# Seven half products in place of eight for three quarters of an MLP's first matrix

## The chip, the cores and the metric

The kernel runs on one core of one Trainium2 chip. A core has TensorE (matrix products, from SBUF into PSUM), VectorE and ScalarE (elementwise work on SBUF and PSUM), GpSimd (elementwise work on SBUF) and SyncE, which issues most of the transfers from HBM. The metric is device time in microseconds (us), from start to end of one execution; here the median of three runs.

## The reference

Two layers of a decoder trunk over 512 tokens of width 1024, in float32. Each layer has a mixer with four branches, a cross attention into 256 memory tokens, and a squared-ReLU MLP with 4096 hidden channels. The change is in the MLP:

```python
h = rmsnorm(x, norm_mlp[l])
x = x + sq_relu_mlp(h, mlp_w1[l], mlp_w2[l])

def sq_relu_mlp(h, w1, w2):
    return jnp.square(jax.nn.relu(h @ w1)) @ w2      # w1: 1024 x 4096, w2: 4096 x 1024
```

## The kernel before

Activations lie transposed: channels in 8 tiles of 128 partitions (index k), the 512 tokens along the free axis. Each matrix product in float32 is made of three in a reduced format (fp32r). Every operand is split into a high half and the low rest, and a product is high by high, high by low and low by high. A product is one weight load of 128x128 and one matmul that streams 512 columns.

**Blocks and units.** All large matrices go through one ring of 9 weight units (`RING`, L151). A unit holds 256 rows by 256 columns, as four squares of 128x128, and comes with one transfer of 256 KB, issued by SyncE when the unit nine earlier has been used (`wait_for_place`, L470). ScalarE writes the unit's high half (`feed`, L1322), GpSimd subtracts it from the raw unit in place, in two instructions (L637, L638), and TensorE uses both (`parts`, L647). A block is four units: it makes two output tiles of 128 channels by 512 tokens in the two banks of a PSUM set, G[0] or G[1], which the blocks take in turn. A unit of a block is 12 products, a block 48. Before the first product of a block TensorE waits until both banks of its set were released (`gemm_free`).

**The MLP** is cut into four quarters of 1024 hidden channels. Block `up{q}_{c}` makes two hidden tiles of quarter q, block `down{q}_{c}` adds quarter q's share to two tiles of x. The order is up0, up1, down0, up2, down1, up3, down2, down3, of four blocks each (L131). The norm's factor per token is not applied to the operands `h_hi` and `h_lo`, but to the hidden tiles: VectorE takes max(product, 0) times the factor into `UPX[0]` (L2533), ScalarE squares it into `UPX[1]` and copies it to the high half (L1798, L1799), VectorE makes the low half (L2537). The factor itself is there only after the first block: TensorE sums the squares behind up0_0 (L1268), ScalarE makes the factor of it (`factors(2)`, L1784). The results of `down` blocks are added to x by VectorE (`residual`, L2419).

**What sets the order.** Each engine has its own queue, written out by hand, and works it off in order. ScalarE feeds weight units in the gaps of its other work: ahead of the two outputs of block b it feeds up to five units (`LEAD`, L153) past that block's last (`feed_past`, L1330). Each instruction of VectorE and ScalarE waits for the one before it on its own engine.

Of the kernel before, what the change touches and what calls it, by code (L numbers as in the profile page):

```python
# [115 lines left out]
def block_order():  # L116
# [14 lines left out]
    order += ups[0] + ups[1] + downs[0] + ups[2] + downs[1] + ups[3] + downs[2] + downs[3]  # L131
# [32 lines left out]

def is_last(u):
    name, part = UNITS[u]
    return part == units_of(name) - 1
# [16 lines left out]
    s5_y_done=2, s5_glu_done=2, s5_ge_value=2, s5_ge_high=2, attn_sc_done=4, attn_pt_done=8, attn_o_done=8, rstd_ready=8, hi_ready=24,  # L184
# [3 lines left out]
    mlstm_mex_ready=1, mlstm_within=4, s5_xp_zero=2, s5_ct_ready=2, s5_bt_ready=4, s5_sq=2, s5_tanh=2,  # L188
    s5_val_ready=2, mghi_ready=8, attn_mm_hi=8, sq_ready=24, attn_kqv_hi=20, attn_kt_ready=8, attn_q_ready=8, attn_vm_ready=4,
    attn_p_exp=16, attn_pt_hi=8, attn_pt_ready=8, attn_ohi_ready=8, up_relu=32, up_hi=32, hx_ready=8, h_ready=24, hg_decay_ready=5,  # L190
# [3 lines left out]
    s5_cp_ready=2, s5_xp_ready=2, s5_kk_ready=6, s5_cl_ready=1, s5_x_ready=1, s5_ys_ready=2, s5_poly=2, s5_ge_ready=2,  # L194
# [5 lines left out]
def build(nc, ins, out):  # L200
# [7 lines left out]
    with ctx:  # L208
# [5 lines left out]
        Hhi = sb("h_hi", [P, KC, SEQ], F32R)  # L214
        Hlo = sb("h_lo", [P, KC, SEQ], F32R)
        merged_at = nc.sbuf_base
# [85 lines left out]
        gemm_free = [sem(f"gemm_free{i}") for i in range(2)]  # L302
# [67 lines left out]
        def ones_and_values(rows, t, h):  # L370
# [43 lines left out]
                   "cl_ready", "u_ready", "w_done", "u4_in", "x_ready", "y_done", "ge_value", "ge_high", "ys_ready", "sq", "poly", "tanh",  # L414
# [35 lines left out]
        MHID = [[YS_R[:, 16 * b + 8 * p:16 * b + 8 * p + 8, :] for p in range(2)] for b in range(2)]  # L450
# [19 lines left out]
        def wait_for_place(eng, u):  # L470

            layer, unit = divmod(u - RING, NUNIT)
            if is_last(unit):
                n = layer * NBLOCK + BLOCK["g_v" if UNITS[unit][0] == "r_i" else UNITS[unit][0]]
                eng.wait_ge(gemm_done[n % 2], 2 * (n // 2) + 2)
            else:
                eng.wait_ge(unit_used, INNER[u - RING])
# [164 lines left out]
        def _(pe):  # L642
# [4 lines left out]
            def parts(name, hi, lo, kind="fm", n=SEQ, ready=None, ready_at=0):  # L647
# [5 lines left out]
                if used:  # L653
                    pe.wait_ge(gemm_free[s], 2 * used)
                u0, units, kcs = first_unit(name), units_of(name), 1 if kind == "wide" else 2
                for un in range(units):
# [4 lines left out]
                    for reg in range(nt):  # L661
                        for k in range(kcs):
# [37 lines left out]
            def token_values():  # L700
# [18 lines left out]
                if used0:  # L719
                    pe.wait_ge(gemm_free[s0], 2 * used0)  # L720
# [3 lines left out]
                if used1:  # L724
                    pe.wait_ge(gemm_free[s1], 2 * used1)
# [189 lines left out]
            for L in range(DEPTH):  # L915
# [254 lines left out]
                pe.wait_ge(gemm_free[s], 2 * used)  # L1170
# [93 lines left out]
                for q in (0, 1):  # L1264
                    for c in range(4):
                        gemm(f"up{q}_{c}", *H, ready=h_ready if (q, c) == (0, 0) else None, ready_at=16)
                        if (q, c) == (0, 0):
                            norm(2)  # L1268

                def down(q):  # L1270
                    hb = MHID[q % 2]
                    for c in range(4):
                        gemm(f"down{q}_{c}", lambda k: hb[0][:, k, :], lambda k: hb[1][:, k, :],
                             ready=uplo if c == 0 else None, ready_at=8 * q)

                down(0)
                for c in range(4):
                    gemm(f"up2_{c}", *H)
                down(1)
                for c in range(4):  # L1280
                    gemm(f"up3_{c}", *H)
                down(2)
                down(3)

# [10 lines left out]
            for t in (0, 1):  # L1295
                n = DEPTH * NBLOCK - 2 + t
                pe.wait_ge(gemm_free[n % 2], 2 * (n // 2) + 2)
# [17 lines left out]
        def _(act):  # L1315
# [6 lines left out]
            def feed(upto):  # L1322

                for u in range(fed[0], min(upto, ALL_UNITS)):
                    act.wait_ge(raw_in[u % RING], COME[u])
# [57 lines left out]
            def values_out(name):  # L1383
                s, used = psum_set(name)
                for b in range(2):
# [5 lines left out]
                    act.nop().then_inc(gemm_free[s], 1)  # L1391

            def banks(name):
# [3 lines left out]
                for b in range(2):  # L1397
                    act.wait_ge(gemm_done[s], 2 * used + b + 1)
                    yield b, G[s][b], gemm_free[s]
# [14 lines left out]
            def gate(n, c):  # L1414
# [3 lines left out]
                for b in range(2):  # L1418
# [4 lines left out]
                    act.nop().then_inc(gemm_free[s], 1)  # L1423
# [1163 lines left out]
```

## Time and profile before

| | us |
|---|---|
| median of three runs (1978.82 to 1979.11) | 1979.01 |
| the profiled execution's own time | 1979.01 |
| its span, first to last instruction | 1977.2 |
| TensorE busy | 1954.3 (99%) |
| GpSimd busy | 1086.8 (55%) |
| VectorE busy | 959.0 (49%) |
| ScalarE busy | 913.8 (46%) |

Busy time is the union of the instructions' spans. A matmul's span includes its fill and drain and overlaps the next one's, so that the distance of two starts, not the span of one, is what a matmul costs. "Idle before, releaser" names what ended an engine's idle time. The MLP of layer 0 runs from about 643 to 991 us, that of layer 1 from about 1615 to 1963 us.

### The profile page before, as it was taken

How to read it: one execution, taken by the hardware profiler on the slowest of the kernel's cores; microseconds unless marked ns; L12 is line 12 of the kernel's file. 1: busy time of each engine (PE TensorE's matmuls, PEld its weight loads, DVE VectorE, ACT ScalarE, POOL GpSimd, SP SyncE). 2: the span in 40 equal slices, each digit the busy share in tenths (PEclk: the TensorE clock that was granted, in tenths of full speed). 3: DMA queues.
4: the chain of work that ended last, by engine and by line, in shares of the span. 5: the costliest groups of instructions: out<-in, count | busy, mean ns of one | idle time of the engine just before them, and what ended most of it. 6: DMA issues, size and time to landing. Idle time of an engine off the chain costs nothing.

```text
span 1977.2 us, 30720 instructions
## 1 busy us (share of the span) xinstructions
PE 1954.3 (99%) x11859; PEld 1619.5 (82%) x11859; DVE 959.0 (49%) x1430; ACT 913.8 (46%) x1560; POOL 1086.8 (55%) x1356
## 2 busy tenths in 40 slices
PE   7999999999999999999999999999999999999998
PEld 6778788888888888888887877888798888888887
DVE  5887778856153321211258787786631532211212
ACT  6754645345454542333355546353554544333323
POOL 5565564946835454546464555368585445545451
PEclk9999999999999999999999999999999999999999
DMA  6323333333422333333333233233343233333331
GB/s 188 110 74 86 81 81 87 91 104 112 142 86 81 97 97 96 96 96 98 99 97 81 70 86 81 75 91 86 118 136 110 75 95 97 96 96 97 98 99 70
DMA packets 197262, 190.72 MB, mean 96 GB/s; under 512 B 23738, under 2 KB 190204, under 8 KB 196732
## 3 DMA queue, kind: packets, MB, share of 16 engines
q1 hardware_dynamic: 196252, 186.66, 32.5%
q8 instruction: 94, 1.54, 0.3%
q10 hardware_dynamic: 864, 2.10, 0.3%
q14 instruction: 52, 0.43, 0.1%
HBM read 184.51 MB, written 3.15 MB: 95 GB/s over the span
## 4 chain that ended last, share of the span: by engine, by line
PE 95%; ACT 2%; DVE 2%; issue 0%; DMA 0%; POOL 0%; SPq 0%; DVEq 0%; ACTq 0%
PE gemm L644 87%; PE mix L644 7%; DVE work L1826 1%; ACT w_hi L1327 1%; PE mix L1223 0%; DVE h_lo L1835 0%; DVE work L1835 0%; DMA work<-in_norm_mix_dram 0%; DVE gate_t L1835 0%; PE mix L885 0%; ACT work L1492 0%; PE mix L1119 0%; ACT work_split L1485 0%; DVE work L2217 0%; ACT work L1447 0%
## 5 line engine op out<-in xcount | busy, mean ns | idle before, releaser
L637 POOL TENSOR_TENSOR w_lo<-w_raw,w_hi 128x256 fp32r<-128x256 f32 x676 | 567.2, 839 | 862.3 <-ACT w_hi L1327 861.9
L644 PE MATMUL gemm<-work_split,w_hi 128*128 128x512 f32 (+1 forms) x2064 | 604.2, 377 | 2.8 <-ACTq L1423 2.8
L638 POOL TENSOR_TENSOR w_lo<-w_raw,w_hi 128x256 fp32r<-128x256 f32 x676 | 571.3, 845 | 0.0
L644 PE MATMUL gemm<-h_hi,w_hi 128*128 128x512 f32 x1440 | 568.6, 395 | 1.1 <-DVE h_lo L1835 1.1
L644 PE MATMUL gemm<-h_lo,w_hi 128*128 128x512 f32 x1440 | 560.9, 389 | 0.0
L644 PE MATMUL gemm<-h_hi,w_lo 128*128 128x512 f32 x1440 | 560.8, 389 | 0.0
L1327 ACT ACTIVATE w_hi<-w_raw 128x512 fp32r<-128x512 f32 x676 | 384.7, 623 | 232.2 <-DMA w_raw<-in_mlp_w_dram 186.2
L644 PEld LDWEIGHTS gemm<-work_split,w_hi 128*128 128x128 f32 x2064 | 378.6, 188 | 74.2 <-ACTq L1423 3.7
L644 PE MATMUL gemm<-work_split,w_lo 128*128 128x512 f32 (+1 forms) x1032 | 388.0, 376 | 0.0
L644 PEld LDWEIGHTS gemm<-h_hi,w_hi 128*128 128x128 f32 x1440 | 270.3, 188 | 65.7 <-issue 6.6
L644 PEld LDWEIGHTS gemm<-h_hi,w_lo 128*128 128x128 f32 x1440 | 270.3, 188 | 57.1
L644 PEld LDWEIGHTS gemm<-h_lo,w_hi 128*128 128x128 f32 x1440 | 270.5, 188 | 55.0 <-issue 1.0
L1826 DVE TENSOR_TENSOR x_t<-x_t,gemm 128x512 f32<-128x512 f32 x96 | 66.0, 687 | 356.6 <-PE gemm L644 355.6
L644 PEld LDWEIGHTS gemm<-work_split,w_lo 128*128 128x128 f32 x1032 | 194.3, 188 | 35.4
L1835 DVE SCALAR_TENSOR_TENSOR gate_t<-gemm,work 128x512 f32<-128x512 f32 x64 | 44.3, 692 | 183.7 <-PE gemm L644 166.8
L1798 ACT ACTIVATE gate_t<-gate_t 128x512 f32<-128x512 f32 x64 | 40.5, 632 | 190.9 <-DVE gate_t L1835 190.9
L1826 DVE TENSOR_TENSOR work<-work 128x512 f32<-128x512 f32 (+5 forms) x134 | 120.4, 899 | 14.1 <-ACT work L1528 6.5
L1422 ACT ACTIVATE gate_t<-gemm 128x512 f32<-128x512 f32 x52 | 31.1, 599 | 141.1 <-PE gemm L644 140.7
L644 PEld LDWEIGHTS mix<-work 64*64 64x64 f32 (+4 forms) x3136 | 76.9, 129 | 17.7 <-issue 14.4
L1835 DVE SCALAR_TENSOR_TENSOR work_split<-gate_t,work_split 128x512 fp32r<-128x512 f32 x64 | 45.4, 710 | 88.9 <-ACT work_split L1799 88.9
L644 PE MATMUL mix<-work 64*64 64x64 f32 (+8 forms) x3136 | 84.2, 231 | 0.9 <-DVE work L1835 0.6
L644 PE MATMUL gemm<-w_hi,work_split 128*128 128x512 f32 x192 | 66.1, 398 | 1.5 <-POOL w_lo L638 1.5
(318 smaller groups left out, 1643.6 us busy)
## 6 DMA issues: line engine op xcount, KB each, us to landing
w_raw<-in_mlp_w_dram SPq DMA_DIRECT2D x256, 256.0 KB, 2.7
w_raw<-in_w_in_dram SPq DMA_DIRECT2D x208, 256.0 KB, 2.7
w_raw<-in_xattn_w_kv_dram SPq DMA_DIRECT2D x64, 256.0 KB, 3.0
w_raw<-in_w_branch_dram SPq DMA_DIRECT2D x32, 256.0 KB, 2.6
w_raw<-in_w_out_dram SPq DMA_DIRECT2D x32, 256.0 KB, 2.6
w_raw<-in_xattn_w_q_dram SPq DMA_DIRECT2D x32, 256.0 KB, 2.8
w_raw<-in_xattn_w_o_dram SPq DMA_DIRECT2D x32, 256.0 KB, 2.7
w_raw<-in_w_in_dram SPq DMA_DIRECT2D x32, 128.0 KB, 4.1
```

The costliest lines, as they stand in the source:

```text
L637: pool.tensor_tensor(lo[:, 0:half], raw[:, 0:half], hi[:, 0:half].bitcast(F32), ALU.subtract)
L638: pool.tensor_tensor(lo[:, half:], raw[:, half:], hi[:, half:].bitcast(F32), ALU.subtract).then_inc(split_ready, 1)
L644: return pe.matmul(o, w, a, start=start, stop=stop, skip_group_check=True)
L1327: act.activation(hi, raw, ACT.Copy).then_inc(split_hi, 1)
L1422: do(act.activation(t[:, b, :], G[s][b][:, :], ACT.Tanh, scale=0.5), th_ready)
L1798: do(act.activation(UPX[1], UPX[0], ACT.Square), up_a)
L1826: do(dve.tensor_tensor(o, a, b, op), s)
L1835: do(dve.scalar_tensor_tensor(out=o, in0=a, scalar=sc, in1=b, op0=op0, op1=op1), s)
```

## The change

For quarters one to three of the first matrix, a unit's 256x256 square of weights and the matching 256 channels by 512 tokens of the operand are each taken as 2x2 blocks, and their product is made by Winograd's form of Strassen's algorithm: seven products of half the columns (256 tokens each) in place of eight. Each is still three matmuls in fp32r. Sums over the four units of a block are kept in the four banks of the PSUM tensor `mix` (M[0] to M[3]), the results are put together once a block. Quarter zero is made as before.

- **Token operands** (once a layer, TMhi/TMlo and TXhi/TXlo): for each pair j of channel tiles VectorE multiplies x by the gain and the norm factor (two instructions of 512) and makes four sums of 256 (`turned_sums`); ScalarE copies 1024 and 768 elements into the high half (`turned_hi`); VectorE makes the low half, 1024 and 768 elements (`turned_low`). The four pairs are worked in with the hidden tiles 0 to 4 of quarter zero (`TURNS`).
- **Weight operands** (each unit of the 12 blocks): four sums of 128 elements on VectorE (`weight_sums`), one of them in place; a ScalarE copy of 384 elements ahead of the unit's own copy; a VectorE split of 384 (`sums_low`).
- **Outputs** (each of the 12 blocks): a ScalarE copy of 256 from M[0], six VectorE additions (`products_out`), then ReLU, square and high half on ScalarE for each of two tiles, low halves on VectorE.
- **Order**: after quarter zero the blocks alternate, up1_0, down0_0, up1_1, down0_1 and so on, and four `down3` blocks end the layer.
- **Release** of PSUM banks has one semaphore for each bank. TensorE waits for the second bank only ahead of the first product that goes into it. Four semaphores of a part of the mixer (`s5`) are merged into two, with the same waits.

```diff
-    order += ups[0] + ups[1] + downs[0] + ups[2] + downs[1] + ups[3] + downs[2] + downs[3]
+    order += ups[0]
+    for q in range(1, 4):
+        for c in range(4):
+            order += [ups[q][c], downs[q - 1][c]]
+    order += downs[3]
...
+        TURNS = [1, 2, 3, 4]
+        SUM_STEPS = [(q, c) for q in range(1, 4) for c in range(4)]
...
# TensorE, parts(): one wait for each bank
-                if used:
-                    pe.wait_ge(gemm_free[s], 2 * used)
+                        if used and un == 0 and reg * 2 % nt == 0:
+                            pe.wait_ge(gemm_free[s][reg * 2 // nt], used)
...
# TensorE, a block of quarters one to three
+                def up_sums(q, c):
+                    s, used = psum_set(f"up{q}_{c}")
+                    for b in range(2):
+                        pe.wait_ge(gemm_free[s][b], used)
+                    u0 = first_unit(f"up{q}_{c}")
+                    for j in range(4):
+                        u = u0 + j
+                        pe.wait_ge(split_ready, u + 1)
+                        pe.wait_ge(*of_layer(ws_split, sum_unit(u % NUNIT) + 1))
+                        if (q, c) == (1, 0):
+                            pe.wait_ge(*of_layer(h_ready, 24 + j + 1))
...
+                        for n, (o, (w_hi, w_lo), (t_hi, t_lo), opens) in enumerate((
+                                (M[0][:, FIRST], w(0), t(0, FIRST), True), (M[0][:, SECOND], ws(1), tx(1), False),
...
+                            mm(o, w_hi, t_hi, start=opens and j == 0, stop=False)
+                            mm(o, w_hi, t_lo, start=False, stop=False)
+                            i = mm(o, w_lo, t_hi, start=False, stop=j == 3)
...
# ScalarE, feed(): a unit of the twelve blocks waits for its sums
+                    d = sum_unit(u % NUNIT)
+                    if d is None:
+                        act.wait_ge(raw_in[u % RING], COME[u])
+                    else:
+                        act.wait_ge(*of_layer(ws_ready, d + 1))
+                        act.activation(SWhi[d % 4], SWraw[d % 4], ACT.Copy)
                     raw, hi, _ = unit_at(u)
                     act.activation(hi, raw, ACT.Copy).then_inc(split_hi, 1)
...
# ScalarE, the MLP
+                def turned_hi(j):
+                    act.wait_ge(*of_layer(hx_ready, 8 + j + 1))
+                    do(act.activation(TMhi[:, 2 * j:2 * j + 2, :], TMraw[:, 2 * j:2 * j + 2, :], ACT.Copy))
+                    do(act.activation(TXhi[j], TXraw[j], ACT.Copy), hi_ready)
...
+                for c in range(4):
+                    feed(min(first_unit(f"up0_{c}") + 4 + LEAD, first_unit("up1_0")))
+                    if c == 3:
+                        feed(first_unit("up1_0") + 4)
+                    for b in range(2):
+                        act.wait_ge(*of_layer(up_v, n + 1))
+                        if n:
+                            act.wait_ge(*of_layer(uplo, n))
+                        do(act.activation(UPX[1], UPX[0], ACT.Square), up_a)
+                        do(act.activation(MHID[0][0][:, 2 * c + b, :], UPX[1], ACT.Copy), uphi)
+                        n += 1
+                        if n in TURNS:
+                            turned_hi(TURNS.index(n))
+                feed_past("up1_0")
+                feed(first_unit("down0_0") + 4)
+                for t, (q, c) in enumerate(SUM_STEPS):
+                    ahead = first_unit("up{}_{}".format(*SUM_STEPS[t + 1])) if t < 11 else first_unit("down3_0")
+                    if t < 11:
+                        feed(ahead + 3)
+                    s, used = psum_set(f"up{q}_{c}")
+                    act.wait_ge(gemm_done[s], 2 * used + 2)
+                    do(act.activation(UPX[0][:, FIRST], M[0][:, FIRST], ACT.Copy), up_a)
+                    feed(ahead + 4)
...
+                    if t < 11:
+                        feed(ahead + 8)
...
# VectorE, the MLP
+                def weight_sums(u):
+                    dve.wait_ge(raw_in[u % RING], COME[u])
+                    d = sum_unit(u % NUNIT)
+                    if d >= 4:
+                        wait_used(dve, u - 8)
...
+                ahead = first_unit("up1_0")
+                for c in range(4):
+                    s, used = psum_set(f"up0_{c}")
+                    if c == 3:
+                        for j in range(4):
+                            weight_sums(ahead + j)
+                            if j:
+                                sums_low(ahead + j - 1)
+                        sums_low(ahead + 3)
+                    for b in range(2):
+                        dve.wait_ge(gemm_done[s], 2 * used + b + 1)
+                        if n:
+                            dve.wait_ge(*of_layer(up_a, n))
+                        stt(UPX[0], G[s][b][:, :], 0.0, R(32)[:, 0, :], ALU.max, ALU.mult, up_v)
+                        dve.nop().then_inc(gemm_free[s][b], 1)
+                        if n in TURNS:
+                            turned_low(TURNS.index(n))
+                        n += 1
+                        if n in TURNS:
+                            turned_sums(TURNS.index(n))
+                        hidden_low(0, c, b, UPX[1])
+                for t, (q, c) in enumerate(SUM_STEPS):
+                    if t:
+                        residual("down{}_{}".format(SUM_STEPS[t - 1][0] - 1, SUM_STEPS[t - 1][1]))
+                    ahead = first_unit("up{}_{}".format(*SUM_STEPS[t + 1])) if t < 11 else None
+                    if ahead:
+                        weight_sums(ahead)
+                        weight_sums(ahead + 1)
+                        sums_low(ahead)
+                        weight_sums(ahead + 2)
+                        sums_low(ahead + 1)
+                    products_out(q, c, n)
+                    if ahead:
+                        weight_sums(ahead + 3)
+                        sums_low(ahead + 2)
+                    hidden_low(q, c, 0, MHRAW[q % 2][:, 2 * c, :])
+                    if ahead:
+                        sums_low(ahead + 3)
+                    hidden_low(q, c, 1, MHRAW[q % 2][:, 2 * c + 1, :])
```

## Rows read from the trace of the kernel before

**Rows 1.** The page, part 1 (busy us, share, instructions) and part 4 (last chain).

```profile
PE 1954.3 (99%) x11859; PEld 1619.5 (82%) x11859; DVE 959.0 (49%) x1430; ACT 913.8 (46%) x1560; POOL 1086.8 (55%) x1356
...
PE 95%; ACT 2%; DVE 2%; issue 0%; DMA 0%; POOL 0%; SPq 0%; DVEq 0%; ACTq 0%
```

**Rows 2.** The waits of TensorE: total us, times, longest us.

```profile
PE gemm L905 <- DMA work<-in_norm_mix_dram: 7.0, 1, 7.0
PE gemm L644 <- ACTq L1423: 2.8, 2, 1.4
```

**Rows 3.** The timeline of TensorE, 533 to 536: start, us, instruction, count.

```profile
533.03 0.39 PE L644 MATMUL gemm<-h_hi,w_hi 128*128 128x512 f32 x1
...
535.75 0.39 PE L644 MATMUL gemm<-h_hi,w_hi 128*128 128x512 f32 x1
```

**Rows 4.** The timeline of VectorE, the MLP's first blocks of layer 0.

```profile
656.08 0.69 DVE L1835 SCALAR_TENSOR_TENSOR gate_t<-gemm,work 128x512 f32<-128x512 f32 x1 [7.89 <-ACT work L1359]
...
664.25 0.69 DVE L1835 SCALAR_TENSOR_TENSOR gate_t<-gemm,work 128x512 f32<-128x512 f32 x1 [2.54 <-PE gemm L644]
666.31 1.60 DVE L1835 SCALAR_TENSOR_TENSOR work_split<-gate_t,work_split 128x512 fp32r<-128x512 f32 x1 [1.36 <-ACT work_split L1799]
```

**Rows 5.** The timeline of ScalarE, the same blocks.

```profile
656.87 0.63 ACT L1798 ACTIVATE gate_t<-gate_t 128x512 f32<-128x512 f32 x1 [0.88 <-DVE gate_t L1835]
...
661.02 2.20 ACT L1327 ACTIVATE w_hi<-w_raw 128x512 fp32r<-128x512 f32 x4
```

**Rows 6.** The timeline of GpSimd, the same blocks.

```profile
661.73 0.75 POOL L637 TENSOR_TENSOR w_lo<-w_raw,w_hi 128x256 fp32r<-128x256 f32 x1 [8.78 <-ACT w_hi L1327]
662.43 0.75 POOL L638 TENSOR_TENSOR w_lo<-w_raw,w_hi 128x256 fp32r<-128x256 f32 x1
```

**Rows 7.** Busy us in one stretch of the MLP: PE, PEld, DVE, ACT, POOL; clock, DMA.

```profile
700.00:800.00 100.00, 100.00 (x443) 82.80 (x442) 19.99 (x30) 35.18 (x59) 50.88 (x72) 1.00 0.32 96
```

**Rows 8.** The timeline of TensorE, attention of layer 0.

```profile
551.39 0.28 PE L644 MATMUL mix<-work_split,merged_split 128*128 128x256 f32 x1
...
553.42 0.28 PE L644 MATMUL mix<-work_split 128*128 128x256 f32 x1
```

**Rows 9.** The timeline of VectorE and GpSimd, 190 to 206, in the mixer.

```profile
190.92 3.39 DVE L1835 SCALAR_TENSOR_TENSOR work<-work,params_all 128x512 f32<-128x512 f32 x3
191.44 1.18 POOL L638 TENSOR_TENSOR w_lo<-w_raw,w_hi 128x256 fp32r<-128x256 f32 x1
...
193.73 1.19 POOL L638 TENSOR_TENSOR w_lo<-w_raw,w_hi 128x256 fp32r<-128x256 f32 x1
...
197.34 0.43 DVE L1826 TENSOR_TENSOR work<-work 128x256 f32<-128x256 f32 x1
...
198.84 0.69 DVE L1826 TENSOR_TENSOR work<-work 128x512 f32<-128x512 f32 x1
...
200.15 2.33 DVE L1835 SCALAR_TENSOR_TENSOR work<-work,params_all 128x512 f32<-128x512 f32 x3
```

**Rows 10.** Groups of ScalarE by form: busy us, mean ns, idle before.

```profile
L1428 ACT ACTIVATE work<-work 128x1024 f32<-128x1024 f32 x12 | 12.7, 1062 | 27.0 <-DVE work L1826 26.9
```

**Rows 11.** TensorE at both ends (timeline), then the granted clock (windows; column PEclk).

```profile
11.77 1.09 PE L885 MATMUL mix<-consts_sb,work 128*128 128x128 f32 x4 [0.86 <-ACT work_split L1485]
...
14.84 0.62 PE L644 MATMUL gemm<-w_lo,work_split 128*128 128x512 f32 x1
15.27 0.42 PE L644 MATMUL gemm<-w_hi,work_split 128*128 128x512 f32 x1
...
15.76 0.39 PE L644 MATMUL gemm<-w_lo,work_split 128*128 128x512 f32 x1
15.99 0.39 PE L644 MATMUL gemm<-w_hi,work_split 128*128 128x512 f32 x1
...
1969.11 0.33 PE L1289 MATMUL mix<-consts_sb,merged 128*128 128x128 f32 x1 [0.36 <-ACT small L1811]
...
1970.00:1972.00 2.00, 0.00 (x0) 0.00 (x0) 2.00 (x4) 1.39 (x3) 0.00 (x0) 0.79 0.48 193
```

More of the change, by code:

```diff
@@ L162, in units_of, with sum_unit @@
     return 1 if name.startswith("branch") else 2 if name == "glu" else 8 if name.startswith("val") or name == "r_i" else 0 if name == "g_v" else 4
+def sum_unit(u):
+    name, part = UNITS[u]
+    return 16 * (int(name[2]) - 1) + 4 * int(name[4]) + part if name.startswith("up") and name[2] != "0" else None
 def is_last(u):
@@ L467, in chained, with wait_used @@
             return do
-        def wait_for_place(eng, u):
-            layer, unit = divmod(u - RING, NUNIT)
+        def wait_used(eng, u):
+            layer, unit = divmod(u, NUNIT)
             if is_last(unit):
@@ L1287, in turned, with down @@
+                def down(q, c):
+                    hb = MHID[q % 2]
+                    gemm(f"down{q}_{c}", lambda k: hb[0][:, k, :], lambda k: hb[1][:, k, :],
+                         ready=uplo if c == 0 else None, ready_at=8 * q)
+                for q, c in SUM_STEPS:
+                    up_sums(q, c)
+                    down(q - 1, c)
+                for c in range(4):
+                    down(3, c)
             def turned(k, ts):
@@ L1296, in _ @@
                 n = DEPTH * NBLOCK - 2 + t
-                pe.wait_ge(gemm_free[n % 2], 2 * (n // 2) + 2)
+                for b in range(2):
+                    pe.wait_ge(gemm_free[n % 2][b], n // 2 + 1)
                 for k in range(6):
@@ L2540, in down @@
-                def down(q):
-                    for c in range(4):
-                        residual(f"down{q}_{c}", norm=3 if q == 3 else None)
-                    if q == 3:
-                        if now[0] < DEPTH - 1:
-                            unscaled_low("norm_mix", 7, 1)
-                            add_squares(3, 7, 8)
-                up(0)
-                up(1)
-                down(0)
-                up(2)
-                down(1)
-                up(3)
-                down(2)
@@ new lines, in sums_low, with products_out @@
+                def sums_low(u):
+                    d = sum_unit(u % NUNIT)
+                    dve.wait_ge(split_hi, u + 1)
+                    stt(SWlo[d % 4], SWraw[d % 4], 1.0, SWhi[d % 4].bitcast(F32), ALU.mult, ALU.subtract, ws_split)
+                def products_out(q, c, n):
+                    s, used = psum_set(f"up{q}_{c}")
+                    y1, y2 = (MHRAW[q % 2][:, 2 * c + b, :] for b in range(2))
+                    first, both = UPX[0][:, FIRST], UPX[0][:, SECOND]
+                    dve.wait_ge(gemm_done[s], 2 * used + 2)
+                    dve.wait_ge(*of_layer(up_a, 8 + 4 * (q - 1) + c + 1))
+                    tt(both, first, M[0][:, SECOND], ALU.add)
+                    tt(y1[:, FIRST], first, M[1][:, FIRST], ALU.add)
+                    tt(y1[:, SECOND], both, M[1][:, SECOND], ALU.add)
+                    tt(y1[:, SECOND], y1[:, SECOND], M[2][:, SECOND], ALU.add, up_v)
+                    tt(both, both, M[3][:, FIRST], ALU.add)
+                    tt(y2.rearrange("p (a t) -> p a t", a=2), M[2].rearrange("p (a t) -> p a t", a=2), bc(both, 1, 2), ALU.add, up_v)
+                    for b in range(2):
+                        dve.nop().then_inc(gemm_free[s][b], 1)
@@ L2557, in _ @@
+                residual("down2_3")
+                for c in range(4):
+                    residual(f"down3_{c}", norm=3)
+                if now[0] < DEPTH - 1:
+                    unscaled_low("norm_mix", 7, 1)
+                    add_squares(3, 7, 8)
             dve.wait_ge(p_act, PRO_ACT + 2)
```

181 lines of the change are left out of this document (100 added, 81 removed).

## The prediction

> **What bounds the kernel now.** I read the page first: TensorE is busy 99% of the span, and the chain that ended last runs 95% through it [rows 1]. The waits of TensorE come next: the longest is 7.0 us, once, at the start, and the others are under 3 us [rows 2]. So whatever takes TensorE time in the MLP shows one for one, and whatever makes it wait there is new. Third, the timeline of matmul starts, because busy spans overlap: thirteen 512-column products start from 533.03 to 535.75, so one costs 2.72/12 = 0.2267 us [rows 3]. Fourth, the first quarter of the MLP on VectorE, ScalarE and GpSimd: only this says how much room the others have just where the change puts work [rows 4 to 6]. Over the MLP VectorE is 20%, ScalarE 35%, GpSimd 51% busy [rows 7].
>
> **What the change removes.** In 12 of 16 `up` blocks a layer, 48 products of 512 columns (48 x 0.2267 = 10.88 us) become 4 x 7 x 3 = 84 of 256 columns. Attention has such products, each with its own weight load: 18 starts from 551.39 to 553.42 give 2.03/17 = 0.1194 us [rows 8]. 84 x 0.1194 = 10.03 us. Saved: 0.85 us a block, 10.2 us a layer, 20.4 us in all: 7.8% of a block and not an eighth, since about 13 ns come with each product whatever its width (226.7 = 213.3 + 13.4, 119.4 = 106.7 + 12.7). *By the Trainium skill ("TensorE: Matmul & The Clock Gate", Back-to-back issue gap) a warm product takes N/2.4 + 2.5 ns, so 215.8 and 109.2 ns: a block would save 10.36 - 9.17 = 1.19 us, 28 us in all. The trace does not agree (226.7 and 119.4), and I go by the trace.*
>
> **Prices of the new elementwise work.** VectorE with two SBUF operands takes 0.43 us at 256 elements and 0.69 at 512, 0.03 more to the next start; with the per-channel vector 2.33/3 = 0.78 from start to start [rows 9]. The slope, 1.04 ns an element, gives estimates of 0.29 us at 128, 0.56 at 384, 0.96 at 768, 1.22 at 1024. ScalarE: 0.63 at 512 and 1.06 at 1024 [rows 5, 10], hence 0.52 at 384 and 0.84 at 768; a weight unit 2.20/4 = 0.55 [rows 5]. GpSimd: 0.70 an operation, 1.4 a unit [rows 6]. Where both GpSimd and VectorE work on SBUF, three such VectorE instructions take 3.39 instead of 2.33 us, and GpSimd starts every (193.73 - 191.44)/2 = 1.14 instead of 0.70 us [rows 9, 6]: they alternate, and each collision costs VectorE 0.36 us (1.13 - 0.78). A VectorE instruction that reads PSUM is not held (0.69 at 664.25 with GpSimd active [rows 4, 6]). *The Trainium skill ("GPSIMD Engine Reference", the table's line on SBUF interfaces) says the interfaces are shared when VectorE has two SBUF inputs; that speaks against this change, and these rows agree.* Bounds per collision: 0 if GpSimd is never active at that moment, 0.91 from one row (1.60 instead of 0.69 at 666.31 [rows 4]); I take 0.36, of which there are several rows.
>
> **Quarter zero, where the new work lands** (layer 0's clock; layer 1 runs the same program and is taken to repeat it). VectorE cannot begin before 656.1: it waits for the norm factor [rows 4, 5]. TensorE finishes the blocks up0_1, up0_2, up0_3 at about 665.4, 676.3 and 687.3 (the last wait of a block's first tile ends 1.4 before, 664.25 [rows 4]).
> - `turned_sums(0)`: 2 x 0.78 + 4 x 0.46 = 3.4, to 660.2. Split and next ReLU, 2 x 0.72, to 661.7. ScalarE's `turned_hi(0)` (1.06 + 0.84) to 662.2, `turned_low(0)` (1.25 + 0.99) to 664.5, `turned_sums(1)` to 667.9, `turned_hi(1)` to 669.9.
> - Only now does ScalarE feed weight unit 9 (before: at 661.02 [rows 5]). High half at 670.4; both GpSimd halves wait for the long instructions of `turned_low(1)`, ready at 673.3. TensorE wants it one unit into up0_2, at 668.1. **Wait 5.3 us** (4.0 without collisions).
> - `turned_low(1)` ends 672.5, `turned_sums(2)` 3.4 + 6 x 0.36 with one more, 677.9; split and ReLU 679.7; `turned_hi(2)`, `turned_low(2)` 682.2; `turned_sums(3)` 685.6; `turned_hi(3)` 687.6. Then units 13 to 15 are fed, the first ready at 691.1 against 684.3 when TensorE wants it. **Wait 6.8** (4.6 without collisions).
> - up0_3 ends at 691.1 + 8.2 = 699.3, 12 late. The first weight sums (4 x 0.32) end at 695.8, ScalarE 697.0, GpSimd 698.8: in time.
> - The four sums and splits (7.5 and seven collisions) stand before up0_3's tiles on VectorE, to 704.7; ScalarE's last copy of them is at 709.7, and only then is down0_0 fed, ready 712.3, while up1_0 ends at 709.4. **Wait 3.0.**
>
> Together 15.1 us a layer (10.3 without collisions) against 10.2 saved.
>
> **The steady step.** TensorE: 10.03 + 10.88 = 20.9 us. The elementwise chain, behind from the start: residual 1.4, three weight sums and two splits 5.0, ScalarE's unit and the copy of the first product 1.0, `products_out` 3.0, fourth sum 1.3, its ScalarE copies 1.1, two times ReLU, square, copy 4.0, last split 0.7, six hand-overs of 0.1: 18.2, and five collisions 1.8: 20.0. It keeps pace with 0.9 us to spare; with nine collisions it takes 21.4 and TensorE waits 0.5 in each of 22 steps. The ring of nine lets a unit of the next `up` in when the unit nine earlier is used, over ten us ahead of need, and DMA stays hidden. The new order of blocks issues the same transfers. The releases of single banks give at most a few tenths, TensorE having no such waits now [rows 2].
>
> **The clock.** At the end it is still full when the last product starts at 1969.11, and in the window from 1970 to 1972 its mean is 0.79: it fell at about 1971.2, under 2 us after the last product [rows 11]. At the start, after seven idle us and one more wait, 512-column products start every 0.43 us (1.2 GHz) until 15.27 and then every 0.23. From 11.77 that is 3.5 us at half rate: 1.75 lost. Three new waits a layer are all longer than 2 us: cost 0 (none falls) to 6 x 1.75 = 10.5; I take 4, between none and half, for the closing stretch was thin already before it stopped.
>
> **The sum.** 2 x (15.1 - 10.2) + 4 = +14 on the profiled run's 1979.0 (its span 1977.2 and 1.8 around it; it is also the median): 1993.
>
> **Rivals.**
> 1. *The step becomes the bound.* Nine collisions, or dearer short instructions (128-element operations have no row; 16 a step, so 0.05 each is 0.8 us). About 1 us over in each of 22 steps: +22, 2015. For: 0.9 of slack only. Against: it is summed from quiet rows and partly hidden.
> 2. *The new waits only eat the saving.* No collisions, the clock never falls: 10.3 against 10.2, so 1979. For: many rows are quiet. Against: GpSimd's burst is fed exactly as VectorE's dense part begins.
> 3. *Faster.* The half product is cheap: the 13 ns go by columns, not by instruction, so 226.7/2 = 113.3 ns, in the place of all 2016 of them. Saving 16.3 us a layer against 10.3 to 15.1 of waits: 1967 to 1977, say 1972. With all the waits above it decides at (10.88 - 15.1/12)/84 = 0.1146 us. For: attention's products are short groups. Against: seventeen equal steps of 0.1194 in them. *The Trainium skill's rule above would save 28 us: 1979 + 21 - 28 = 1972 without collisions, 1985 with all waits and the clock.*
>
> Chances: forecast 0.45 (1985 to 2003 by itself), rival one 0.22, two 0.15, three 0.14, something else 0.04. An unmoved time means within 0.2%, 4 us, which is what a measurement can tell here: 0.08; faster 0.17, slower 0.75. The range leaves one in ten at either side: 1972 to 2018.
>
> **What would show it.** Per layer three waits of TensorE inside quarter zero and before down0_0, of 5, 7 and 3 us, released by GpSimd's `w_lo`; 256-column starts 0.119 apart in `up1_0`; about 20.9 us from one `up` block to the next and no wait from up1_1 on; VectorE's 128-element instructions at 0.29, or 0.65 where GpSimd is active; a granted clock under 1 in layer parts only near those waits. It is wrong if the feed of unit 9 comes before 668, if the step is above 21, or if the half products start 0.113 apart.

## The result, and the profile after

The changed kernel takes 2018.7 us (median of four runs, 2018.05 to 2018.98) against 1979.06 (1978.82 to 1980.55) of the kernel before, run beside it: ratio 1.0199, with a 95% interval of 1.0186 to 1.0212. It is 39.6 us slower. The forecast was 1993, range 1972 to 2018: the sign was right, the size was not, and the time lies just above the range.

The page of the changed kernel, parts 1 and 4, as in [rows 1]:

```profile
PE 1950.9 (97%) x12723; PEld 1649.4 (82%) x12723; DVE 1323.5 (66%) x2070; ACT 1004.1 (50%) x1744; POOL 1107.1 (55%) x1356
...
PE 66%; DVE 21%; ACT 10%; issue 2%; DVEq 0%; DMA 0%; POOL 0%; SPq 0%; ACTq 0%
```

TensorE's share of the last chain fell from 95% to 66%; VectorE and ScalarE hold 31% of it. The waits of TensorE (total us, times, longest us) name a new releaser, `DVEq`, and one that has grown: GpSimd's `w_lo` ended one wait of 1.5 us in the kernel before and ends seven now:

```profile
PE gemm L675 <- POOL w_lo L669: 24.2, 7, 5.2
PE mix L675 <- DVEq L2663: 21.5, 22, 1.6
...
PE gemm L675 <- ACTq L1487: 1.4, 2, 0.7
```

The first line is quarter zero and the wait before down0_0 (but for one wait of 1.2 us elsewhere). The second is the release of the `mix` banks, once in each of the 22 steps (11 a layer; a step is one `up` block of half products and the `down` block behind it). The third was 2.8 us in [rows 2] and is now half of that: the two banks of this set are released 0.7 us apart, and TensorE now starts behind the first. Each wait on the timeline of TensorE (start, us, instruction; in brackets the idle time before it and its releaser), first the three of layer 0 that the prediction placed, then one step:

```profile
667.15 0.39 PE L675 MATMUL gemm<-h_hi,w_lo 128*128 128x512 f32 x1
672.61 0.80 PE L675 MATMUL gemm<-h_hi,w_hi 128*128 128x512 f32 x1 [5.07 <-POOL w_lo L669]
...
685.87 0.39 PE L675 MATMUL gemm<-h_hi,w_lo 128*128 128x512 f32 x1
690.76 0.50 PE L675 MATMUL gemm<-h_hi,w_hi 128*128 128x512 f32 x1 [4.51 <-POOL w_lo L669]
...
713.05 0.70 PE L675 MATMUL gemm<-work_split,w_hi 128*128 128x512 f32 x2 [2.12 <-POOL w_lo L669]
...
768.92 0.39 PE L675 MATMUL gemm<-work_split,w_lo 128*128 128x512 f32 x1
770.15 0.48 PE L675 MATMUL mix<-work_split,w_hi 128*128 128x256 f32 x2 [0.85 <-DVEq L2663]
...
780.30 0.63 PE L675 MATMUL gemm<-work_split,w_hi 128*128 128x512 f32 x2
...
790.99 0.39 PE L675 MATMUL gemm<-work_split,w_lo 128*128 128x512 f32 x1
792.23 0.47 PE L675 MATMUL mix<-work_split,w_hi 128*128 128x256 f32 x2 [0.86 <-DVEq L2663]
```

What a wait costs is the distance of two starts less a product: 5.46 - 0.23 = 5.23, then 4.66, 2.28, and 1.0 to 1.8 before each `up` block. The step shown is 792.23 - 770.15 = 22.08 us, of which 84 half products take 10.15 (0.1208 each) and 48 whole ones 10.88.

The clock is a third item. Windows of the changed kernel (stretch, its length, busy us of PE, PEld, DVE, ACT, POOL, then PEclk, DMA share, GB/s) around the first two waits and the third:

```profile
672.00:673.50 1.50, 0.89 (x2) 0.79 (x3) 1.46 (x2) 0.69 (x2) 1.50 (x2) 0.50 0.00 0
676.50:678.00 1.50, 1.50 (x5) 1.13 (x5) 1.43 (x3) 0.17 (x1) 1.50 (x3) 0.55 0.00 0
678.00:679.50 1.50, 1.50 (x8) 1.20 (x7) 1.47 (x2) 1.47 (x2) 0.33 (x1) 1.00 0.19 48
690.50:691.50 1.00, 0.74 (x3) 0.64 (x4) 0.97 (x2) 0.00 (x0) 1.00 (x2) 1.00 0.00 0
691.50:693.00 1.50, 1.50 (x6) 1.12 (x5) 0.48 (x1) 0.90 (x2) 1.50 (x3) 0.51 0.00 0
694.50:696.00 1.50, 1.50 (x7) 1.18 (x7) 1.35 (x5) 0.12 (x1) 0.00 (x0) 0.86 0.00 0
713.00:717.00 4.00, 3.95 (x17) 3.30 (x18) 3.79 (x7) 1.05 (x2) 4.00 (x6) 1.00 0.01 3
```

From 672.61 to 677.89 twelve products of 512 columns take 5.28 us and not 2.72: 2.6 lost. From 690.76 to 694.99 eleven take 4.23 and not 2.49: 1.7 lost. The wait before 713.05 cost no clock here.

**The account.** Waits: layer 0 12.2 in quarter zero and before down0_0, 12.5 in the steps; layer 1 (the same places on its timeline) 11.7 and 12.5; together 49.0 before rounding. Clock: 4.3 and, from the same count in layer 1, 1.85 + 2.95 = 4.8; together 9.1. Two small terms: the waits for ScalarE's release are 1.4 shorter, and a block of 84 half products takes 10.15 us where it begins behind a wait, against 10.07 where it does not (experiments 3 and 4), 1.7 in 22 blocks. Saving, measured by itself in experiment 1: 18.1 by the time, 19.1 by the two MLPs on the timeline (that execution's first product waited 0.7 longer for its data). 49.0 + 9.1 - 1.4 + 1.7 - 19.1 = 39.3 (40.3 with 18.1), against 39.6 measured.

### The profile page after: what moved, and what is told of

Its sections match the earlier page's. It is cut to its first block, busy times and chain, and to the rows that moved or that the text cites. A ratio compares the mean times of both kernels' runs of the same rounds, so it can differ in the third digit from the quotient of the medians.

```text
span 2016.7 us, 33624 instructions
## 1 busy us (share of the span) xinstructions
PE 1950.9 (97%) x12723; PEld 1649.4 (82%) x12723; DVE 1323.5 (66%) x2070; ACT 1004.1 (50%) x1744; POOL 1107.1 (55%) x1356
## 4 chain that ended last, share of the span: by engine, by line
PE 66%; DVE 21%; ACT 10%; issue 2%; DVEq 0%; DMA 0%; POOL 0%; SPq 0%; ACTq 0%
PE gemm L675 57%; DVE work L1914 8%; PE mix L675 8%; DVE w_raw L1914 3%; DVE work_split L1923 2%; ACT w_hi L1391 2%; DVE h_raw L1914 1%; DVE x_t L1914 1%; ACT gate_rows L1389 1%; DVE s_phases L1914 1%; DVE gate_t L1914 1%; DVE work L1923 1%; ACT h_raw L1884 1%; ACT h_hi L1885 1%; DVE h_lo L1923 1%
## 5 line engine op out<-in xcount | busy, mean ns | idle before, releaser
L675 PE MATMUL gemm<-h_lo,w_hi 128*128 128x512 f32 x1312 | 514.6, 392 | 0.0
L675 PE MATMUL gemm<-h_hi,w_lo 128*128 128x512 f32 x1312 | 514.0, 392 | 0.0
L675 PE MATMUL gemm<-work_split,w_hi 128*128 128x512 f32 (+1 forms) x1552 | 447.1, 373 | 4.4 <-POOL w_lo L669 3.0
L675 PEld LDWEIGHTS gemm<-work_split,w_hi 128*128 128x128 f32 x1552 | 281.4, 188 | 55.3 <-issue 3.7
L675 PE MATMUL gemm<-work_split,w_lo 128*128 128x512 f32 (+1 forms) x776 | 288.4, 372 | 0.0
L675 PEld LDWEIGHTS gemm<-work_split,w_lo 128*128 128x128 f32 x776 | 146.2, 188 | 25.4
L1914 DVE TENSOR_TENSOR work<-work 128x256 f32<-128x256 f32 (+5 forms) x160 | 134.8, 842 | 14.9 <-ACT work L1592 6.5
L675 PE MATMUL mix<-work_split,w_hi 128*128 128x256 f32 (+1 forms) x544 | 122.5, 289 | 21.5 <-DVEq L2663 21.5
L675 PEld LDWEIGHTS mix<-work_split,w_hi 128*128 128x128 f32 x544 | 90.3, 191 | 30.9 <-DVEq L2663 30.2
L675 PE MATMUL mix<-work_split,gate_rows 128*128 128x256 f32 x504 | 103.5, 283 | 0.0
```

Of the source, the lines that this page charges most:

```text
L675: return pe.matmul(o, w, a, start=start, stop=stop, skip_group_check=True)
L1914: do(dve.tensor_tensor(o, a, b, op), s)
```

## Experiments

The saving and the order are taken alone, on the kernel before; then the steady step and quarter zero of the changed kernel are varied. Three or more rounds each.

**1. The half products alone.** In the kernel before, the twelve blocks issue 84 products of 256 columns on operands that are there anyway. Left out: the sums on both sides and the right values of these blocks.

```diff
+                        for n in range(7):
+                            o = G[s][n // 4][:, 256 * (n % 4 // 2):256 * (n % 4 // 2) + 256]
...
+                            mm(o, WHi[:, u % RING, cols], Hhi[:, k, half], start=opens, stop=False)
+                            mm(o, WHi[:, u % RING, cols], Hlo[:, k, half], start=False, stop=False)
+                            i = mm(o, WLo[:, u % RING, cols], Hhi[:, k, half], start=False, stop=j == 3)
```

> The kernel before with TensorE's part of the change alone: in the 12 blocks a layer of quarters one to three, 84 products of 256 columns in place of 48 of 512, on the operands that are there (no sums, so the block's values are left out). Theory (a half product costs 0.1208 us as in the changed kernel's trace, 10.15 us a block against 10.88): 24 x 0.73 = 17.5 us less, 1961.5. Rival one (the skill's 109.2 ns and the forecast's 0.1194): 1951 or 1958.6. Rival two (half products bring nothing inside a long block because of weight loads): 1979.

Measured 1960.64 (1960.38 to 1961.18) beside 1978.77: ratio 0.9908, interval 0.9891 to 0.9925. The saving is 18.1 us, 0.75 a block (0.79 by its MLPs alone), where the prediction had 0.85. Its products, on TensorE's timeline of this run:

```profile
697.80 0.28 PE L644 MATMUL gemm<-h_hi,w_lo 128*128 128x256 f32 x1
697.92 0.28 PE L644 MATMUL gemm<-h_hi,w_hi 128*128 128x256 f32 x1
```

They start 0.12 apart: a product has its fixed part at half the width too. I had expected 1961.5 (a saving of 17.5). The cheap half product of rival three (0.1133) is ruled out.

**2. The order of blocks alone.** The kernel before with `up` and `down` alternating: in the order of the weight units, on TensorE and on VectorE (ScalarE's hidden tiles keep their order).

```diff
+                for q in range(1, 4):
+                    for c in range(4):
+                        gemm(f"up{q}_{c}", *H)
+                        down(q - 1, c)
```

> The kernel before with the new block order alone (up and down blocks in turn). Theory: the order costs nothing, 1979 within 2. Rival (the order itself makes waits: each up block's outputs have one down block's time, and weights come in another order): a wait like the 1.0 us a step of the changed kernel, 22 to 25 us more, 2002.

Measured 1978.83, ratio 1.0001 (0.9991 to 1.001). The order costs nothing.

**3. Short subtractions on GpSimd.** In the changed kernel, from up1_0 on, GpSimd subtracts only 16 of 256 columns in each half unit, and TensorE reads the high half where it read the low. Left out: most of the low halves of the weights. VectorE and ScalarE do all that they did.

```diff
-                half = raw.shape[-1] // 2
+                half, name = raw.shape[-1] // 2, UNITS[u % NUNIT][0]
+                if name[:2] == "up" and name[2] != "0" or name[:4] == "down":
+                    pool.tensor_tensor(lo[:, 0:16], raw[:, 0:16], hi[:, 0:16].bitcast(F32), ALU.subtract)
+                    pool.tensor_tensor(lo[:, half:half + 16], raw[:, half:half + 16], hi[:, half:half + 16].bitcast(F32), ALU.subtract).then_inc(split_ready, 1)
+                    continue
```

> The changed kernel, with GpSimd's two subtractions a unit cut to 16 columns each from up1_0 on (the low halves of those weights are left out; TensorE reads the high half in their place, as many products). VectorE and ScalarE do all their work. Theory (collisions with GpSimd, about 11 a step at 0.42, put the step above TensorE's 21.05): the eleven waits a layer vanish, and part of the wait before down0_0, 2018.7 - 25 = 1994. Rival (the chain is that long by itself, VectorE's short instructions and its waits for ScalarE): the waits stay, 2014 to 2019.

Measured 1988.29 (1987.13 to 1989.15), ratio 1.0046 (1.0032 to 1.0061): 30.4 us under the changed kernel. Of the new waits only the two of quarter zero are left (5.23 and 4.64 in layer 0). The forecast was 1994, since I had expected only a part of the wait before down0_0 to go (3.4 us in two layers); most of the rest is the 0.075 us a block by which half products are faster without a wait in front. The edit also shortens GpSimd's own work, not its collisions alone. That can explain the wait before down0_0, which ended with GpSimd's low half, but hardly the step waits, which ended with VectorE's release, in a chain of VectorE and ScalarE in which neither waits for GpSimd. VectorE's timeline in the changed kernel and, second, in this run, both in a step:

```profile
774.58 0.69 DVE L1923 SCALAR_TENSOR_TENSOR h_lo<-h_raw,h_hi 128x512 fp32r<-128x512 f32 x1 [2.50 <-ACT h_hi L1885]
...
777.30 1.52 DVE L1914 TENSOR_TENSOR x_t<-x_t,gemm 128x512 f32<-128x512 f32 x2
779.04 0.47 DVE L1914 TENSOR_TENSOR work<-w_raw 128x128 f32<-128x128 f32 x1 [0.22 <-DVE x_t L1914]
779.54 0.71 DVE L1914 TENSOR_TENSOR work<-work,w_raw 128x128 f32<-128x128 f32 x1
780.29 0.72 DVE L1914 TENSOR_TENSOR w_raw<-w_raw 128x128 f32<-128x128 f32 x1
781.04 0.71 DVE L1914 TENSOR_TENSOR work<-w_raw,work 128x128 f32<-128x128 f32 x1
...
785.36 0.29 DVE L1914 TENSOR_TENSOR work<-w_raw 128x128 f32<-128x128 f32 x1
...
789.01 0.42 DVE L1914 TENSOR_TENSOR gate_t<-gate_t,mix 128x256 f32<-128x256 f32 x1 [0.89 <-ACT gate_t L1878]
```

```profile
781.78 0.69 DVE L1927 SCALAR_TENSOR_TENSOR h_lo<-h_raw,h_hi 128x512 fp32r<-128x512 f32 x1 [2.50 <-ACT h_hi L1889]
...
784.51 1.52 DVE L1918 TENSOR_TENSOR x_t<-x_t,gemm 128x512 f32<-128x512 f32 x2
787.28 0.29 DVE L1918 TENSOR_TENSOR work<-w_raw 128x128 f32<-128x128 f32 x1 [1.25 <-DMA w_raw<-in_mlp_w_dram]
```

The same short instructions take 0.71 us, most of them, in the one and 0.29 in the other, and in the second the engine is early enough to wait for the weights. The wait of 2.50 us for ScalarE is in both: the chain through ScalarE stands in every step, and what makes the chain longer than TensorE's work is the collisions on top of it. ScalarE's copies and GpSimd's own timeline in the changed kernel show why there are so many:

```profile
776.51 2.20 ACT L1391 ACTIVATE w_hi<-w_raw 128x512 fp32r<-128x512 f32 x4
...
777.22 0.75 POOL L668 TENSOR_TENSOR w_lo<-w_raw,w_hi 128x256 fp32r<-128x256 f32 x1 [3.06 <-ACT w_hi L1391]
...
780.06 0.78 POOL L668 TENSOR_TENSOR w_lo<-w_raw,w_hi 128x256 fp32r<-128x256 f32 x1
780.82 0.78 POOL L669 TENSOR_TENSOR w_lo<-w_raw,w_hi 128x256 fp32r<-128x256 f32 x1
```

ScalarE feeds four units back to back from 776.51, GpSimd then subtracts without a pause until 784.6, and just there VectorE has its weight sums. VectorE's starts (779.54, 780.29, 781.04) are then 0.75 apart, as GpSimd's are: one short instruction of VectorE passes for each of GpSimd's, and the rest of the time it is held.

**4. Hidden tiles first.** The changed kernel with ScalarE's work for both hidden tiles ahead of the fourth unit's copies, and VectorE's split of that unit's sums last.

```diff
                     do(act.activation(UPX[0][:, FIRST], M[0][:, FIRST], ACT.Copy), up_a)
-                    feed(ahead + 4)
                     for b in range(2):
...
+                    feed(ahead + 4)
...
# VectorE
                     hidden_low(q, c, 0, MHRAW[q % 2][:, 2 * c, :])
+                    hidden_low(q, c, 1, MHRAW[q % 2][:, 2 * c + 1, :])
                     if ahead:
                         sums_low(ahead + 3)
-                    hidden_low(q, c, 1, MHRAW[q % 2][:, 2 * c + 1, :])
```

> The changed kernel, but in each step ScalarE makes both hidden tiles before it feeds the fourth weight unit, and VectorE splits them before that unit's sums. All work stays. Theory (the step of 22.1 us is the chain of VectorE and ScalarE, of which VectorE idles 2.5 and 0.7 us behind that feed; 2 us of it go): TensorE is the bound again at 21.05, the eleven waits of 1.0 to 1.75 us a layer vanish, 2018.7 - 24 = 1995, the three waits of quarter zero stay. Rival (VectorE is full with its own work and collisions): 2018 within 3. Rival two (the waits come from GpSimd's lows or the ring): 2018 too.

Measured 1995.61 (1995.18 to 1996.36), ratio 1.0085 (1.007 to 1.01): 23.1 us are back, as expected. The waits of TensorE in this run, and then VectorE's residual in two steps that follow each other:

```profile
PE gemm L675 <- POOL w_lo L669: 25.5, 8, 5.4
...
PE mix L675 <- DVEq L2663: 3.2, 2, 1.6
```

```profile
771.00 1.52 DVE L1914 TENSOR_TENSOR x_t<-x_t,gemm 128x512 f32<-128x512 f32 x2
...
791.15 1.52 DVE L1914 TENSOR_TENSOR x_t<-x_t,gemm 128x512 f32<-128x512 f32 x2
```

Of 22 waits for `DVEq` two are left, the first step of each layer. The collisions did not go (128-element instructions still take 0.71 in the step), but VectorE now waits 0.4 us for ScalarE where it waited 3.2, and its cycle is 20.15 us in place of 22.08, under TensorE's 21.0. So the excess of the step has two parts, either of which removes it: ten collisions, or the weight unit that ScalarE copies ahead of the hidden tiles.

**5. One pair of token operands.** In the changed kernel TMhi to TXlo are made for the first of four pairs only, and all blocks use that pair.

```diff
+                    if j:
+                        do(dve.nop(), hx_ready)
+                        return
```

> The changed kernel, with the token operands made for the first of four pairs only and used for all (the other three pairs' operands are left out; TensorE's work is the same). Theory: the two waits of 5.2 and 4.7 us in quarter zero and their half-rate clock (2.6 + 1.6 us) go, 2018.7 - 2 x 14 = 1990.5; the 2.3 us before down0_0 and the steady waits of 1 us stay. Rival (the waits come from the weight sums of up1_0 or the feed's order alone): they move to up1_0, 2005 to 2018.

Measured 1989.14 (1988.86 to 1989.39), ratio 1.0051 (1.0034 to 1.0067). The two waits in quarter zero are gone, so the token operands make them. One of 2.2 us before down0_0 and ten of 1.0 a layer stay; the eleventh, before up1_1, is gone. Waits and saving give 1979.1 - 18.1 + 2 x (2.2 + 10.3) = 1986.0, 3.1 too few. In the profiled execution the clock fell after the wait before down0_0. This run's windows, and the last instruction of VectorE before the release that up1_1 waits for:

```profile
699.00:700.00 1.00, 0.68 (x3) 0.62 (x4) 0.96 (x2) 0.19 (x1) 1.00 (x3) 1.00 0.37 128
700.00:704.00 4.00, 4.00 (x13) 3.10 (x12) 3.79 (x7) 1.25 (x3) 4.00 (x6) 0.57 0.00 0
```

```profile
711.10 0.69 DVE L1917 TENSOR_TENSOR h_raw<-mix,gate_t 128x512 f32<-128x512 f32 x1
```

A mean of 0.57 over 4 us is 1.7 us lost, 3.4 in two layers, which closes the sum (the two small terms of the account nearly cancel here). But it is not a cost of its own. TensorE reached up1_1 at 711.94, when the banks (read until 711.79) had just been released; 1.7 us earlier it would have waited for them, as it does in the changed kernel (1.76). The four executions say the same: their mean clocks were 0.996, 0.997, 0.999 and 0.999 and their times 1989.4, 1989.2, 1989.1 and 1988.9. A mean of 0.999 is about 2 us lost in all and leaves room for one such stretch at most, yet these two are shorter by half a us at most. A wait of the same length in the changed kernel (2.28, before 713.05) cost no clock.

**6. Feed first in quarter zero.** The changed kernel with the next block's weight units fed ahead of the token copies of pairs 2 and 4.

```diff
+                        if n in (2, 4):
+                            feed(min(first_unit(f"up0_{n // 2}") + 4 + LEAD, first_unit("up1_0")))
                         if n in TURNS:
```

> The changed kernel, with ScalarE feeding the next block's weight units before the high halves of token pairs two and four, not after them. Theory (VectorE has not the time before up1_0: it ends the first unit's sums at 695.8 whatever the feed does): TensorE runs quarter zero without a wait, ends it at 687 and then waits some 10 us before up1_0: same time within 4, 2018. Rival (the feed's place behind the token operands is the whole cause): both waits and the clock's loss go, 1990 to 1995.

Measured 2020.72 (2019.42 to 2021.99), ratio 1.0211 (1.0195 to 1.0226): no gain, within 3 us of the 2018 expected. The waits moved, but not all to up1_0 as I had thought. In layer 0 they cost 1.99 (release of a bank, at 678.6) and 2.99 (at 683.1), and 6.32 before the first half product:

```profile
692.77 0.39 PE L675 MATMUL gemm<-h_hi,w_lo 128*128 128x512 f32 x1
699.32 0.76 PE L675 MATMUL mix<-work_split,w_hi 128*128 128x256 f32 x2 [6.16 <-POOL w_lo L669]
```

In either of the two orders tried quarter zero does not hold this much work; the order decided which block waits.

**7. One plain block more.** Experiment 4, with up1_0 made as before, and the four pairs of token operands with every second hidden tile over five blocks.

```diff
-        TURNS = [1, 2, 3, 4]
+        TURNS = [1, 3, 5, 7]
...
+                    if (q, c) == (1, 0):
+                        gemm("up1_0", *H)
+                    else:
+                        up_sums(q, c)
```

> e4_hidden_first, and up1_0 is made by the plain eight products, so that 11 blocks a layer have seven; the token operands are made with hidden tiles 1, 3, 5, 7, two blocks' time more to do it. Theory (the quarter-zero waits are a lack of time for VectorE's token operands in front of up1_0): no new waits left, 1979 - 22 x 0.73 = 1963. Rival (the first weight feed stays behind the token operands whatever the room): waits of 2 to 5 us a layer with a clock drop, 1975 to 1985.

Measured 1983.54 (1983.41 to 1984.27), ratio 1.0024 (1.0015 to 1.0033): 20 us above what I expected. It lies in the rival's range, but not for the rival's reason. The waits of quarter zero shrank to 0.4 and 1.0, but VectorE had all four units' sums of up1_1 ahead of the output of up1_0, whose banks up1_1 needs. TensorE, and the VectorE instruction that sets those banks free:

```profile
710.27 0.39 PE L675 MATMUL gemm<-work_split,w_lo 128*128 128x512 f32 x1
718.46 0.77 PE L675 MATMUL mix<-work_split,w_hi 128*128 128x256 f32 x2 [7.80 <-issue]
```

```profile
701.52 0.70 DVE L1918 TENSOR_TENSOR work<-w_raw 128x128 f32<-128x128 f32 x1
...
717.61 0.69 DVE L1927 SCALAR_TENSOR_TENSOR gate_t<-gemm,work 128x512 f32<-128x512 f32 x1
```

The starts of TensorE are 8.19 us apart, and the last bank is read from 717.61 to 718.30. With this wait (8.0 a layer), the two small ones and 8.3 a layer saved, the sum is 1979 + 2 x (9.4 - 8.3) = 1981. The clock was at half until 723.4, 2.5 us lost in layer 0 and 1.7 in layer 1; the shorter waits for ScalarE's release give back 1.4. Together 1984.

**8. Outputs first.** Experiment 7 with the outputs of up1_0 ahead, and the sums of one unit beside each. The edit is shown against experiment 7; ScalarE feeds the four units of up1_1 beside these outputs and behind them.

```diff
# VectorE
-                    if c == 4:
-                        for j in range(4):
-                            weight_sums(ahead + j)
...
+                        if c == 4:
+                            weight_sums(ahead + b)
                         hidden_low(c // 4, c % 4, b, UPX[1])
+                sums_low(ahead)
+                for j in (2, 3):
+                    weight_sums(ahead + j)
+                    sums_low(ahead + j - 1)
+                sums_low(ahead + 3)
```

> e7_one_plain_block, whose trace shows one wait of 8 us a layer in front of up1_1: its first product waits until up1_0's two banks are released, and VectorE takes these behind the sums of all four units of up1_1. Here up1_0's outputs come first, with one unit's sums beside each. Theory (that wait and the half-rate stretch behind it, about 2 us, are all that is between e7 and the saving): 1983.5 - 2 x 10 = 1963, faster than the kernel before by 0.8%. Rival (VectorE has not the time even so, the wait moves to up1_1's weights): 1970 to 1984.

Measured 1966.29 (1965.77 to 1966.85), before 1979.09: ratio 0.9935 (0.9922 to 0.9949), 3 us above the 1963 expected. This is faster than both kernels, by 12.8 us against before and by 52.4 against the changed one. Per layer 0.4, 1.0 and 0.8 us of waits stay; with eleven half-product blocks in place of twelve (8.3 saved a layer) that is 1979.1 - 16.6 + 4.5 = 1967.0, and 1965.6 with the 1.4 of ScalarE's release.

```profile
PE 1939.3 (99%) x12651; PEld 1642.6 (84%) x12651; DVE 1302.9 (66%) x2022; ACT 998.1 (51%) x1730; POOL 1115.1 (57%) x1356
```

## Why the prediction was wrong in size

- **What bounds the kernel: right.** TensorE's time showed one for one (experiment 1), and every new wait did (the account above).
- **The saving: a little high.** 0.85 us a block from attention's rate of 0.1194 [rows 8]; measured 0.75 to 0.79. In long runs half products start 0.120 apart, and 0.121 in a block that begins behind a wait (10.07 and 10.15 us a block). 20.4 forecast, 18.1 measured.
- **Quarter zero: right in its mechanism.** Three waits a layer, where they were placed, 23.9 us in two layers where the forecast had 30.2. VectorE, ScalarE and GpSimd follow the written timeline: the feed of unit 9 was forecast at 669.9 and is at 669.35, that of unit 13 at 687.6 and is at 687.50, on a timeline that runs 0.7 us earlier from the start of the MLP. The six collisions priced into `turned_sums(2)` are there (5.69 us for 1.54 + 1.80 of quiet work), and those of the next pair are not, as forecast:

```profile
672.01 2.24 DVE L1923 SCALAR_TENSOR_TENSOR work<-x_t,params_all,work 128x512 f32<-128x512 f32 x2
674.29 3.45 DVE L1914 TENSOR_TENSOR work<-work 128x256 f32<-128x256 f32 x4
...
682.06 1.54 DVE L1923 SCALAR_TENSOR_TENSOR work<-x_t,params_all,work 128x512 f32<-128x512 f32 x2
683.63 1.80 DVE L1914 TENSOR_TENSOR work<-work 128x256 f32<-128x256 f32 x4
```

- **The clock: mis-sized, but mostly hidden.** The term was 4 us in all; the loss was 9.1. The bound of 10.5 held as a sum, but not its price of 1.75 a wait: 2.6 and 2.95 were lost after single waits, and none after the third. I had taken the thin closing stretch of the kernel as a reason to go low. What I did not see is that time lost at half rate is not added to the next wait: TensorE gets to it later, and the other engines go on (experiment 5 has it too). In layer 0 the first wait is followed by 2.6 lost and a second wait of 4.66, together 7.3; in layer 1 by 1.85 and 5.39, together 7.2. Then 1.7 and 2.28 in layer 0, 2.95 and 1.08 in layer 1: 4.0 both. So quarter zero costs 5.2 + 7.2 + 4.0 = 16.4 us a layer, waits and clock together, where the forecast had 5.3 + 6.8 + 3.0 + 2 = 17.1. Read so, its waits were 1.3 too low, and the 2 for the clock were added where the clock adds nothing: that the sums meet within 1 us is in part luck.
- **The steady step: this is the step that failed.** The prediction put it as "it keeps pace with 0.9 us to spare". Its own sign of being wrong, a step above 21, is met by 22.08. The quiet chain of 18.2 was right: the measured cycle of 22.08 less its collisions (0.18 + 7 x 0.42 + 0.47 + 0.42 = 4.0, from the 128-element instructions from 779.04 to 787.5 over their quiet 0.29) is 18.1. Its five collisions of 0.36, 1.8 in all, were ten, most of them of 0.42, 4.0 in all. Two errors meet there. The price came from a 512-element instruction (1.13 instead of 0.78); a short one is held until GpSimd's next slot, 0.75 after the last. And the number five stands in the prediction without a reason; it goes with GpSimd's share of busy time (51% [rows 7]), though the diff says when that time comes, and the prediction itself says so against rival two. `feed(ahead + 8)` ends ScalarE's turn, so that GpSimd's eight instructions start just ahead of the next weight sums. Experiments 3 and 4 show the cause: without the collisions all 25.1 us of step waits are gone, and without the fed unit in the chain all but 3.6.
- **Rival one was right in its mechanism**, "the step becomes the bound" at about 1 us in each of 22 steps; its price of 22 was 25.1. Without these step waits the measured time would be 2018.7 - 25.1 = 1993.6, where the forecast stood: the other terms hold within 1 us together (2 x 16.4 - 18.1 = +14.7, forecast +14). That they do is in part luck as well: 1.4 less than forecast in waits and clock, and 2.3 less in the saving, nearly cancel.
- **Rivals two and three** fall: the waits of quarter zero ate more than the saving by themselves (23.9 without the clock, against 18.1), and the half product is not cheap.
- **The order** was rightly costed at nothing (experiment 2). `DVEq` waits come from `products_out`, not from the split semaphore.
- **The bank releases** were misread, on a small term. The prediction has "TensorE having no such waits now [rows 2]", but the row `ACTq L1423`, 2.8 us, is one: both banks of a set, freed by ScalarE 0.7 us apart. It is 1.4 in the changed kernel, and the MLP of layer 0 starts 0.7 us earlier by it. No run has this edit alone; experiment 2, which lacks it, still waits 1.39 at that place.

What stays open is why the clock fell after 2.2 us of waiting in one profiled execution of experiment 5 and not in the changed kernel. Not shown either is what makes the half products behind a wait slower by 0.075 us a block.

## What to carry to other kernels

When TensorE's work is cut by giving sums to idle engines, add up the whole cycle from one block's output to the release that the block after next waits for, hand-overs included, and compare it with TensorE's shorter block; a share of busy time says nothing of that. Count collisions from the order of issue: see which instructions of GpSimd are started by what, and what VectorE does in those microseconds. Where the chain is too long by 1 us, moving one weight unit (ScalarE's two copies and VectorE's split) behind the work that the next step waits for brought 23 us, while more of the same in another order (experiment 6) brought nothing, and one more plain block with its outputs first, on top of that move, made the change worth 12.8 us.

## What the chip showed that was not expected

- VectorE's 128-element instruction on two SBUF operands takes 0.29 us alone and 0.71 while GpSimd subtracts; over a stretch of the changed kernel (a group by form, 700 to 960 us: busy us, mean ns, idle before) its mean is in between:

```profile
L1914 DVE TENSOR_TENSOR w_raw<-w_raw 128x128 f32<-128x128 f32 x46 | 28.3, 614 | 1.6
```

  GpSimd is hardly slowed by it (0.75 from start to start, against 0.70 alone), while the 512-element instructions of [rows 9] slow it to 1.14. Here the short instruction pays. The Trainium skill ("GPSIMD Engine Reference", the table's line on SBUF interfaces) names the sharing; these rows agree and add the price.
- The clock can fall after products have started again: after the wait that ended at 690.76 it was full until 691.5 and half until about 695. The waits of 4.7 to 5.4 us cost 1.7 to 3.0 us of clock each, from 4.23 us for eleven products in layer 0 to 6.12 for fourteen in layer 1. What such a loss adds to the time can be less: in experiment 5 it stood where a wait would have been.
- Waits of 1.0 to 1.8 us before each `up` block cost no clock: the windows of 10 us from 720 to 960 all stand at 1.00.
- Half products start 0.1199 apart (84 in 10.07 us) in the blocks of experiments 3 and 4 that TensorE enters without a wait, and 0.1208 (10.15 us) in blocks of the changed kernel, which it enters after a wait of 1 us or more.
